# Expert weights of a mixture-of-experts decoder step: transfers of 2 MB into ten places instead of 1 MB into twenty-one

## What is computed

```python
logits = (xt @ w_router + b_router)
top_v, top_i = lax.top_k(logits, TOP_K)                  # 4 of 32
wts = softmax(top_v)
for e in range(N_EXPERTS):
    z = xt @ w_up[e] + b_up[e]                           # w_up[e]:   1024 x 2048 float32, 8 MB
    gate = minimum(z[:, :1024], 7.0)
    up = clip(z[:, 1024:], -7.0, 7.0)
    act = (up + 1.0) * gate * sigmoid(1.702 * gate)
    out = out + gate_dense[:, e:e+1] * (act @ w_down[e] + b_down[e])   # w_down[e]: 1024 x 1024, 4 MB
```

## Time and profile before

| | |
|---|---|
| Median of 3 runs | 1576.51 us |
| Lowest, highest | 1572.67 us, 1577.09 us |
| Span of the profiled execution | 1575.1 us |
| PE busy | 1447.4 us, 92% |
| DMA mean busy share, rate | 326 GB/s over the whole span |
| Chain that ended last | PE 61%, DMA 29% |
| of it `arena<-in_w_up` (DMA) | 22% |
| of it L1335 and L1365 (PE) | 20% and 9% |
| Granted clock of PE, mean | 0.966 |

### The profile page before, as it was taken

One profiled execution on the slowest core, in us unless ns is written; L12 is line 12 of the kernel. 1 busy time (PEld: TensorE's weight loads), 2 busy tenths in 40 slices (PEclk: granted clock), 3 DMA queues, 4 the chain that ended last, 5 costly groups with the idle time before them and its releaser, 6 DMA issues.

```text
span 1575.1 us, 21206 instructions
## 1 busy us (share of the span) xinstructions
PE 1447.4 (92%) x8595; PEld 656.7 (42%) x8595; DVE 366.8 (23%) x845; ACT 297.0 (19%) x568; POOL 81.6 (5%) x108
## 2 busy tenths in 40 slices
PE   4999999979998969999999999999998998899896
PEld 4565455468876543333333333333332222232221
DVE  5210012346852451101010101011111100110123
ACT  4110004554530211111111111111110110011011
POOL 2000001200000000000000000000000000000000
PEclk9899999978999969999999999999999999999997
DMA  9690775413269579979999999999999999999994
GB/s 277 236 332 30 293 256 196 113 43 137 64 160 298 214 309 384 420 293 421 420 420 420 420 420 420 421 420 421 420 420 420 420 420 421 420 420 419 421 404 173
DMA packets 119927, 513.21 MB, mean 326 GB/s; under 512 B 12946, under 2 KB 42026, under 8 KB 68195
## 3 DMA queue, kind: packets, MB, share of 16 engines
q1 hardware_dynamic: 113090, 489.91, 78.8%
q0 software_dynamic: 6752, 22.06, 4.1%
HBM read 501.06 MB, written 19.22 MB: 330 GB/s over the span
## 4 chain that ended last, share of the span: by engine, by line
PE 61%; DMA 29%; DVE 5%; ACT 2%; SPq 1%; issue 1%; POOL 0%; DVEq 0%; POOLq 0%; ACTq 0%
DMA arena<-in_w_up 22%; PE bank L1335 20%; PE bank L1365 9%; PE bank L1177 4%; PE bank L785 4%; PE bank L1001 3%; PE bank L1002 3%; DMA arena<-in_w_in 2%; PE bank L1270 2%; DMA arena<-in_cache_cmp,arena 2%; PE bank L1327 1%; PE bank L1256 1%; PE bank L1258 1%; PE bank L1350 1%; PE bank L1075 1%
## 5 line engine op out<-in xcount | busy, mean ns | idle before, releaser
L1335 PE MATMUL bank<-arena 128*64 128x512 f32 x2176 | 493.7, 599 | 33.7 <-DMA arena<-in_w_up 33.7
L1335 PEld LDWEIGHTS bank<-arena 128*64 128x64 f32 x2176 | 145.1, 136 | 352.0 <-issue 266.9
L1365 PE MATMUL bank<-arena 128*64 128x512 f32 x1088 | 241.0, 595 | 0.0
L2247 DVE TENSOR_SCALAR arena<-bank,arena 128x1 uint32<-128x1 f32 x34 | 7.4, 219 | 592.3 <-PE bank L1343 592.3
L1365 PEld LDWEIGHTS bank<-arena 128*64 128x64 f32 x1088 | 75.0, 136 | 141.7 <-issue 135.8
L1710 ACT ACTIVATE arena<-arena 128x512 f32<-128x512 f32 x34 | 21.4, 630 | 528.8 <-DVE arena L2250 528.8
L1306 PE MATMUL bank<-arena 128*64 128x512 f32 (+1 forms) x420 | 103.5, 610 | 2.9 <-DVE arena L2208 2.9
L2321 POOL DMA_DIRECT2D slots<-arena x34 | 18.7, 551 | 1179.4 <-ACT arena L1717 1179.4
L1177 PE MATMUL bank<-arena 128*128 128x288 f32 x256 | 74.7, 442 | 2.3 <-DMA arena<-in_w_in 1.4
L2250 DVE TENSOR_SCALAR arena<-bank 128x512 f32<-128x512 f32 x34 | 23.5, 692 | 187.0 <-PE bank L1335 187.0
L1001 PE MATMUL bank<-arena 128*128 128x512 f32 (+1 forms) x112 | 57.0, 589 | 9.2 <-DMA arena<-in_w_in 6.5
(11 more groups left out here) (418 smaller groups left out, 1301.7 us busy)
## 6 DMA issues: line engine op xcount, KB each, us to landing
arena<-in_w_up SPq DMA_DIRECT2D x256, 1024.0 KB, 26.9
arena<-in_w_down SPq DMA_DIRECT2D x128, 1024.0 KB, 26.7
arena<-in_w_ada SPq DMA_DIRECT2D x12, 2048.0 KB, 11.7
arena<-in_w_in SPq DMA_DIRECT2D x6, 2048.0 KB, 13.2
arena<-in_w_in SPq DMA_DIRECT2D x16, 512.0 KB, 4.1
arena<-in_w_out SPq DMA_DIRECT2D x1, 4096.0 KB, 16.9
arena<-slots SPq DMA_DIRECT2D x2, 2048.0 KB, 10.2
out<-in_state_win SPq DMA_DIRECT2D x1, 4064.0 KB
```

The lines of the kernel that those rows point to most:

```text
L1335: last = mm(banks[part][SLOT * s:SLOT * s + SLOT, :], xcT[:, q], ring[n % R_][:, D * part + 512 * s:D * part + 512 * s + 512], start=False ...
L1365: last = mm(banks[4][SLOT * s:SLOT * s + SLOT, :], lhs, ring[n % R_][:, D * v + 512 * s:D * v + 512 * s + 512], start=f == 0, stop=f == 7)
```

## The change

Every transfer of expert weights becomes 2 MB with 16 KB for each partition: a unit of `w_up` gives each partition two neighbouring rows (256 rows in all, 4 units per expert), a unit of `w_down` gives it four (512 rows, 2 units per expert). `PIECES` is 6 x 32 = 192. The ring has ten places of 16 KB per partition, 20 MB where there were 21 MB; the 1 MB place `routed` is dropped. On the first filling SP's waits stand before other units: `out_ps` before unit 3, `y1`, `h2` and `lg_ps` before (and around the store in front of) unit 5, `st_state` before unit 8, `wdiag` before unit 9.

PE does the same matmuls in the same order, but waits once for each unit, before its first half. It still counts 12 halves per chunk in `piece_used`; SP now waits for two counts before each refill. Because a partition holds other rows, the transposes read other columns: those of the next chunk's tokens (L1312) read every second element where they read neighbours, those of the gated values (L1350 before, L1352 after) read every fourth where they read every second.

```diff
-PIECES = 12 * E
+PIECES = 6 * E
...
-        places = ([ring_at + 2 * D * i for i in range(7)] + [x_at - 2 * D] + [ring_at + 2 * D * i for i in range(7, 16)]
-                  + [x_at, spare, spare + 2 * D, routed])
-        ring = [view(a, 2 * D) for a in places]
+        places = [ring_at + 4 * D * i for i in range(8)] + [x_at - 2 * D, spare]
+        ring = [view(a, 4 * D) for a in places]
...
-                e, q = n // 12, n % 12
-                if q < 8:
-                    src = w_up[e, P * q:P * q + P]
-                    dst = ring[n % R_]
+                e, q = n // 6, n % 6
+                if q < 4:
+                    src = w_up[e, 2 * P * q:2 * P * (q + 1)].rearrange("(p k) n -> p k n", k=2)
+                    dst = ring[n % R_].rearrange("p (k n) -> p k n", k=2)
                 else:
-                    src = w_down[e, 2 * P * (q - 8):2 * P * (q - 7)].rearrange("(p k) n -> p k n", k=2)
-                    dst = ring[n % R_].rearrange("p (k n) -> p k n", k=2)
+                    src = w_down[e, 4 * P * (q - 4):4 * P * (q - 3)].rearrange("(p k) n -> p k n", k=4)
+                    dst = ring[n % R_].rearrange("p (k n) -> p k n", k=4)
...
             for n in range(R_):
-                if n == 8:
+                if n == 3:
                     sp.wait_ge(S("out_ps"), 5)
-                if n == 12:
+                if n == 5:
                     sp.wait_ge(S("y1"), 3)
...
-                if n == 17:
+                if n == 8:
                     sp.wait_ge(S("st_state"), 64)
...
-                sp.wait_ge(S("piece_used"), until * 12 + (q + 1))
+                sp.wait_ge(S("piece_used"), until * 12 + 2 * (q + 1))
                 load_piece(n)
...
-                    last = nc.tensor.transpose(banks[2][:, P * k:P * k + P], xr[:, P * k:P * k + P], ident)
+                    last = nc.tensor.transpose(banks[2][:, P * k:P * k + P], xr_pairs[:, k // 2, k % 2], ident)
...
-                        n = 12 * e + q
-                        pe.wait_ge(S(f"ld_piece{n % R_}"), 16 * (n // R_) + 16)
+                        n = 6 * e + q // 2
+                        if q % 2 == 0:
+                            pe.wait_ge(S(f"ld_piece{n % R_}"), 16 * (n // R_) + 16)
```

## The result

The changed kernel takes 1566.37 us (median of 14 runs, 1559.72 to 1570.78), the one before 1573.15 us (14 runs, 1570.46 to 1577.09). The ratio on record is 0.9945, 95% interval 0.9933 to 0.9957: 0.55% faster. The two medians alone give 0.9957, 0.43% faster. Run again beside the experiments it came to 0.9959 (0.9938 to 0.9979). The prediction was 1571.2 us, 0.34% faster, with a range of 1564 to 1583.

A forecast was written before the change was run, and what follows sets the result against it. The prediction took the stream of weights to bound the kernel: ring and release +4.3, last chunk +1.95 and longer packets -11.6 sum to -5.3 us, so 1576.5 becomes 1571.2 us, range 1564 to 1583.

The forecast's parts named there:

- What bounds the kernel: After expert 3's stall: the weight stream sets the end, 2.55 us for 1 MB; PE's earlier gains or losses count nothing.
- First filling: Before the ring is full: the stream rests 5.0 us longer at `out_ps`, but the later stall covers it; no cost.
- A smaller ring and coarser release: At the end of expert 3's stall: 1 MB more to bring, +2.55 us, and a later first release, +1.75 us.
- The last chunk: After the last `w_up` landing: PE has two halves to do, +1.75 us, and wider strides, +0.2 us; in all +1.95 us.
- The wider strides: Transposes reading every second or fourth element take slightly longer; counted once, in the last chunk, +0.2 us.
- `w_down` was covered: In the last chunk: the last 2 MB are wanted 11.2 us after the last `w_up` piece and arrive just in time.
- Longer packets: On the 827 us stretch after the stall: 16 KB packets instead of 8 KB cost 1.4% less, -11.6 us.
- upper bound: For the packet gain after the stall: joining 8 KB packets saves 16 ns of 624, -2.6%, as from 4 to 8 KB.
- The estimate from it: On the stretch after the stall: some 1,300 fewer packets per engine at about 10.5 ns each, 13.6 us gained.
- The sum: Over the whole kernel: 4.3 + 1.95 - 11.6 = -5.3 us, giving 1571.2 us, 0.34% faster.
- Rival (d): Stream rate does not move; only the smaller ring and coarser units count: +6.3 us, 1582.8 us; chance 0.14.

The follow-up runs named there:

- e3: The kernel before with a ring of 17 places of 1 MB instead of 21: ratio 1.0063 to the kernel before.
- e5: The kernel before with six pieces instead of eight loaded ahead of the wait for `out_ps`: ratio 0.9990.
- e1: The changed kernel with its 2 MB transfers and ten places, but runs and packets of 8 KB: ratio 1.0044 to the kernel before.
- e6: The kernel before with runs of 4 KB, still pieces of 1 MB in 21 places: ratio 1.0135.
- e9: The changed kernel with each unit in two 1 MB transfers, to even and to odd partitions, runs of 16 KB: ratio 0.9966 to the kernel before.
- e4: The changed kernel with eight places of 2 MB instead of ten: ratio 1.0040 to the kernel before.
- e7: The changed kernel with 4 MB units, `w_up` in runs of 32 KB, and four places of 4 MB: ratio 1.0125 to the kernel before.
- e2: The changed kernel with each unit in two 1 MB transfers to 64 neighbouring partitions each, runs of 16 KB: 2263.8 us, median of four runs.

## Why the prediction was right

**What bounds the kernel: right.** What the stream had more to bring after the stall came out at the end in full (e3: 10.16 us for 4 MB), and what it lagged behind before the stall did not come out (e3, 4.2 MB behind at 75 us).

**First filling, nothing: right.** The first rest grew from 11.5 to 17 us, and first issue to E3 differs by 0.05 us. The changed kernel is 2 MB behind at 75 us, as the prediction has it, and still finds its ring full before the stall ends. e3 shows the same lag to be free at twice the size; e5 does not, since it catches up before the stall.

**A smaller ring and coarser release, +4.3 us: right in the ring, too high in the release.** e3 gives 2.54 us for a MB (2.55 predicted). SP's refill at the stall comes 1.7 us later (1.75 predicted), but that is not what the stream loses: in its first 20 us from E3 it falls 0.75 us behind. The prediction took the delay of the first refill for the delay of the stream. Together, measured in e1 without the gain, ring and release were 3.3 us and not 4.3.

**The last chunk, +1.95 us: right.** 1.78 us. The wider strides were about as small as taken: the two transposes take 310 and 286 ns for each matmul (308 and 273 in the earlier trace rows). `w_down` was covered. What I had not seen is that the unit before the last would take over as soon as the last one is split.

**Longer packets, -11.6 us: the term that was mis-sized, by 1 us, and the reading behind its upper bound was wrong.** From e1 to the changed kernel the stretch lost 12.7 us, 1.5% where I had 1.4%. The upper bound of 2.6% came from 4 KB against 8 KB, 164 and 312 ns. Read over 300 us the same packets take, with the completion packets counted in:

| packets | share of q1 x 16 x 300 us / packets of weights | ns |
|---|---|---|
| 4 KB (e6) | 1.013 x 4800 / 29629 | 164.1 |
| 8 KB (before) | 1.000 x 4800 / 15213 | 315.5 |
| 16 KB (changed) | 0.993 x 4800 / 7724 | 617.1 |

The window of 2 us from which I took the 312 ns has no completion packet in it at all and begins at a start; it flattered 8 KB. So I made the step from 4 to 8 KB too large (16 ns where it is 13) and that from 8 to 16 KB too small (6 to 9 where it is 14). And these durations overlap a little, by another share at each size, so that the stretch pays only about 9 ns a packet. The shares are good for comparing, the stretch is what is paid. That the -1.4% came so near was in part luck: two windows of some 8 us gave 1.0 and 1.4, and the larger was taken.

The Trainium skill (DMA: Bandwidth & Descriptors, Measured (HBM→SBUF, 128 partitions, SWDGE, issued from GpSimd)) gives about 10.5 ns for each packet. The estimate from it, 13.6 us, missed the measured 12.7 by 0.9 and mine by 1.1, so neither is to be preferred. Nor does the figure's nearness to the 8.7 and 9.8 ns of these runs confirm it: it is the 0.67 us of one 4 KB transfer shared out over its 64 packets, while these runs give a price for each packet of one of 16 engines. The Trainium skill (DMA: Bandwidth & Descriptors, Anatomy of one DMA, SWDGE path) also has a fixed 2.0 us for each DMA. In a full queue these runs show nothing of the kind: e9 issues twice as many transfers as the changed kernel and loses 0.7 us from E3 to L.

**The sum.** In the trace +3.3 + 1.8 - 12.7 = -7.6 us; predicted were +4.3 + 1.95 - 11.6 = -5.3. Two errors of one us, both to the pessimistic side, make the difference between 0.34% and the 0.48% of the trace; the timed runs, 0.43% by the medians and 0.55% by the ratio on record, lie on both sides of that. In absolute time the forecast of 1571.2 was 4.8 us too high, and 3.4 of these are the starting point: the median of the kernel before was 1576.5 us over three runs and is 1573.15 over fourteen. Rival (d), the price without a gain, is what e1 built: I gave it +6.3 us and 1582.8, it took +5.0 us in the trace and 1.0044 in time.

## What to carry to other kernels

When a kernel is bound by a stream of DMA at a flat rate, lengthen the contiguous run of each partition and leave the size of the transfer alone: here 4, 8 and 16 KB gave 409, 420 and 427 GB/s, while 1 MB against 2 MB gave nothing. Price the coarser units at the places where the stream stands still and where it ends, since the rest is covered; look for the next stall that a smaller ring would open (e4, e7). And take a price per packet from a stretch of hundreds of us with everything in it, not from a clean window of 2 us.

## What the runs showed of the hardware

Transfers that go by turns to partitions 0 to 63 and 64 to 127 move at half the rate: e2 held 221 GB/s with all 16 engines busy, e9 with the same bytes and packets, to every second partition, 426 GB/s. Late in e2 the rate rose to 314 GB/s; a likely reason is that engines drifted apart and worked on transfers to both halves at once, but no run tested that. The Trainium skill (SBUF — State Buffer, Door 1: The DMA port swizzle) has the rule: partitions 0 to 63 reach only 8 of 16 ports, about 218 GB/s. The trace agrees, with 221.
